# Another order of the mixer's lists: where panel parts stand between small products

## The reference, cut to what matters

```
h = h + W_out [ HGRN2 heads (4) || sliding-window attention (8 query heads) ](RMSNorm(h))   <- the mixer
h = h + CrossAttention_4heads(RMSNorm(h), RMSNorm(mem))
h = h + W_down relu(W_up RMSNorm(h))^2

HGRN2 per head, in chunks of 64 tokens:
  f = lb + (1 - lb) * sigmoid(f_logit);  k = 1 - f
  scores = sum_k q k decay;  o = q S exp(b) + scores v;  S_new = decay S + k^T v
  out = head_rms(o) * silu(g)
Window attention per head: qk-norm, partial rotary, softmax over 256 keys with a sink, times v
```

## The kernel before

| token | TensorE | ScalarE | VectorE |
|---|---|---|---|
| `\|` | next panel part | with part 0 of panel i: copies the high part of panel i+1 (L1152) | nothing |
| `:` | nothing | takes the next panel's result from PSUM (L1119 to L1143) | nothing |
| `T` | 8 transposes, values and keys (L1601, L1606) | copies both (L1205, L1208) | nothing |
| `s0`..`s3` | scores of two chunks (L1632) | nothing | mask, sum (L1424, L1426) |
| `D`, `S` | `D`: state products (L1615) | nothing | `S`: eight state updates, one after another (L1410, L1416) |
| `o0`..`o3` | output of two chunks (L1646, L1648); o3 needs s3's sum | nothing | nothing |
| `q`, `L`, `E` | `L`: total of squares (L1525) | `q`: square (L1214); `L`: root (L1101 to L1108) | `E`: Newton step, gating (L1271, L1273, L1433, L1436) |
| `n`, `r`, `R` | `n`: total (L1525, L1533) | `n`: root | `r`: Newton step (L1469 ff.); `R`: rotation (L1478, L1480) |
| `g0`..`g8` | nothing | g0, g2, g8 in part (L1169 to L1187) | gates and spans; g8 is L1390, L1392 |
| `c0`..`c3` | c0 and c2: window scores of two each (L1685) | exponentials (L1229, L1233) | scale, mask, minimum (L1491) |
| `x0`..`x3` | nothing | nothing | normalization (L1503, L1505, L1508) |
| `w0`..`w3` | four transposes, "turn" (L1697) | copy (L1241) | nothing |
| `p`, `a` | `p`: attention output (L1707) | `a`: copy out (L1247) | nothing |
| `e0`, `e1` | nothing | e0: out gate (L1193 to L1198) | both (L1397 to L1405) |
| `k` | nothing | next block: square (head 1), high part (head 3, L1090) | sum (head 1, L1286), apply (head 2), low part (head 3) |
| `N` | total for the next block's norm (L1583) | root | nothing |
| `V` | transposes of the window's values (L1658) | copy (L1222) | copy |

## Time and profile before

### The profile page before, as it was taken

How to read it: one execution, slowest core, us unless ns; L and a number is a source line. 1 busy time by engine, 2 the same in 40 slices (tenths; PEclk the granted TensorE clock), 3 DMA queues, 4 the chain that set the end, 5 groups by cost and what they waited for, 6 DMA issues and landing times.

```text
span 2652.0 us, 40225 instructions
## 1 busy us (share of the span) xinstructions
PE 2518.6 (95%) x14110; PEld 2035.9 (77%) x14110; DVE 1736.0 (65%) x3014; ACT 1139.5 (43%) x2164; POOL 895.4 (34%) x1018
## 2 busy tenths in 40 slices
PE   7988899899899889989998999999999999999999
PEld 5767677777777667868777888878888888888887
DVE  6778567667766746566656776787666354556665
ACT  5455455555555535644655322342223223322331
POOL 1432200000000055346424766747665222222222
PEclk9999999999999999999999999999999999999999
DMA  4432443353353343164224344323244953444664
GB/s 184 152 113 82 167 131 100 127 175 99 105 192 113 114 159 111 56 232 174 79 88 163 102 137 167 127 96 123 100 138 162 305 169 104 143 132 147 210 187 143
DMA packets 186562, 371.67 MB, mean 140 GB/s; under 512 B 13936, under 2 KB 79984, under 8 KB 183664
## 3 DMA queue, kind: packets, MB, share of 16 engines
q1 hardware_dynamic: 181200, 359.51, 40.7%
q10 hardware_dynamic: 5152, 9.51, 1.0%
HBM read 286.71 MB, written 79.89 MB: 138 GB/s over the span
## 4 chain that ended last, share of the span: by engine, by line
PE 77%; DVE 10%; issue 5%; ACT 5%; DMA 1%; ACTq 0%; POOL 0%; DVEq 0%; SPq 0%; POOLq 0%
PE bank L3236 8%; PE bank L3238 8%; PE bank L3240 8%; PE bank L3216 7%; PE bank L3212 7%; PE bank L3213 6%; PE bank L1549 5%; PE bank L1559 5%; PE bank L1552 5%; PE bank L2161 3%; PE bank L2166 3%; PE bank L2162 3%; PE bank L1632 1%; PE bank L1707 1%; PE bank L2213 1%
## 5 line engine op out<-in xcount | busy, mean ns | idle before, releaser
L454 POOL TENSOR_TENSOR wlo<-raw,whi 128x256 fp32r<-128x256 f32 x372 | 322.4, 898 | 1084.4 <-ACT whi L1156 613.4
L1549 PE MATMUL bank<-hi,whi 128*128 128x512 f32 x704 | 293.0, 416 | 2.0 <-ACT whi L1152 1.8
L1552 PE MATMUL bank<-lo,whi 128*128 128x512 f32 x704 | 278.2, 395 | 0.0
L3238 PE MATMUL bank<-lo,whi 128*128 128x512 f32 x896 | 275.8, 389 | 0.0
L3236 PE MATMUL bank<-hi,whi 128*128 128x512 f32 x896 | 275.8, 389 | 0.0
L3240 PE MATMUL bank<-hi,wlo 128*128 128x512 f32 x896 | 275.8, 389 | 0.0
L3028 DVE TENSOR_TENSOR lo<-h,hi 128x1024 fp32r<-128x1024 f32 x80 | 124.5, 1557 | 172.9 <-ACT hi L2792 172.9
L2723 POOL TENSOR_TENSOR wlo<-h,whi 128x256 fp32r<-128x256 f32 x160 | 127.4, 820 | 299.7 <-ACT whi L2784 299.7
L2161 PE MATMUL bank<-hi,whi 128*128 128x512 f32 x504 | 207.8, 412 | 12.0 <-DVE h L2054 6.4
L2162 PE MATMUL bank<-lo,whi 128*128 128x512 f32 x504 | 196.9, 391 | 0.0
L3238 PEld LDWEIGHTS bank<-lo,whi 128*128 128x128 f32 x896 | 168.2, 188 | 34.9
(11 more groups left out here) (387 smaller groups left out, 5618.3 us busy)
## 6 DMA issues: line engine op xcount, KB each, us to landing
h<-hidden_scratch SPq DMA_DIRECT2D x96, 512.0 KB, 4.2
raw<-w_mix SPq DMA_DIRECT2D x88, 512.0 KB, 4.1
raw<-w_cross SPq DMA_DIRECT2D x64, 512.0 KB, 3.5
raw<-w_mlp SPq DMA_DIRECT2D x64, 512.0 KB, 4.6
wlo<-mixer_lows_scratch SPq DMA_DIRECT2D x60, 512.0 KB, 3.7
hidden_scratch<-hT SPq DMA_DIRECT2D x116, 256.0 KB, 2.1
h<-w_mlp SPq DMA_DIRECT2D x112, 256.0 KB, 3.0
mixer_lows_scratch<-wlo SPq DMA_DIRECT2D x22, 512.0 KB, 2.9
```

What stands on the lines that cost most here:

```text
L454: last = pool.tensor_tensor(wlo[:, i, cols], raw[:, i, cols], whi[:, i, cols].bitcast(F32), ALU.subtract)
L1549: pe.matmul(out, w, hi[:, k, :], start=k == 0, stop=False)
L1552: pe.matmul(out, w, lo[:, k, :], start=False, stop=False)
L3238: pe.matmul(down_bank(i)[:], wh[:, cols], xl[:, i % 2, :], start=False, stop=False)
```

## The change

Tokens move within and between the strings; none is added or taken away. The order of all other steps, the buffers, banks and semaphores stay. Each panel part and each take (`:`) keeps its number, so a part that stands elsewhere is still the next of the 66.

```diff
-    "head 0": "T | s0 s1 | D | n | S | : | r s2 o0 : | e0 R s3 | o1 e1 : o2 | g0 o3 q",
-    "keys": "V | | g1 L E | n r R : | |",
-    "pair 0": "g2 c0 g3 c1 x0 | g4 x1 g5 | | : w0 w1 g6 c2 | : c3 x2 | w2 g7 | x3 w3 e0 | p a g8 : e1 |",
-    "head 1": "T k s0 s1 | | k D n S k k s2 | | : r o0 k | g0 s3 o1 : o2 k k R g1 k o3 q g2 |",
-    "pair 1": "| N c0 c1 g3 | g4 g5 L | : | x0 x1 E w0 | | : w1 g6 g7 | c2 c3 x2 x3 g8 | w2 w3 e0 : p a e1",
-    "head 2": "T | k s0 s1 k | | D n k S | : r | k s2 o0 k | g0 k R s3 : k g1 o1 o2 o3 k q g2 g3 |",
-    "pair 2": "c0 c1 g4 | | L g5 x0 x1 | : | E | g6 : | w0 c2 | c3 w1 g7 x2 g8 | x3 w2 w3 e0 e1 p : a",
-    "head 3": "k T s0 k k s1 k D n k k S s2 k k r o0 o1 | | s3 | | : g0 | g1 | o2 o3 | R q : g2 g3",
-    "pair 3": "c0 x0 g4 | L | : | c1 | E x1 g5 : g6 | w0 | c2 c3 g7 w1 x2 g8 | | x3 w2 w3 : p a",
+    "head 0": "T | s0 s1 | D n | | S | | : r s2 o0 : s3 | e0 | o1 R e1 : o2 g0 | o3 q",
+    "keys": "V | g1 L | E | n r | R : |",
+    "pair 0": "g2 c0 c1 g3 x0 | | x1 g4 g5 | : w0 w1 g6 c2 | : c3 x2 | w2 g7 | x3 w3 | g8 p e0 a : e1",
+    "head 1": "k T s0 k s1 | | | D n S s2 k k | r o0 k : | k | g0 s3 o1 : o2 R k k | o3 q g1 g2",
+    "pair 1": "| N c0 c1 g3 | L | g4 g5 x0 | : x1 E w0 | | g6 : w1 g7 c2 | c3 x2 x3 g8 | w2 w3 e0 | : p a e1",
+    "head 2": "T k | s0 k s1 | D n k k S | : r | s2 o0 k g0 | k R s3 k g1 o1 : g2 o2 o3 k q g3 |",
+    "pair 2": "c0 c1 g4 | | g5 L x0 x1 | | : E | : | g6 w0 c2 w1 | g7 c3 g8 x2 | x3 w2 w3 e0 e1 p a",
+    "head 3": "k T : s0 k k s1 k k D n k S s2 k k r o0 o1 | | s3 | | : g0 | g1 | o2 o3 | R q : g2 g3",
+    "pair 3": "c0 x0 g4 | | L : c1 | | E x1 g5 : g6 | | w0 c2 c3 g7 g8 x2 w1 | | w2 x3 w3 : p a",
```

## The result

The kernel with the changed lists takes 2628.37 us (median of 4 runs, 2624.63 to 2630.76), the kernel before 2653.26 (4 runs beside it, 2648.4 to 2655.76). The ratio is 0.9903, with an interval of 0.989 to 0.9915: 25 us or 1% faster. The forecast was 2628.

What follows compares the result with a forecast made beforehand. TensorE, busy 95% of the span, bounds the kernel, through gaps and stretches at 1.2 GHz. Terms 7.85 + 5.2 + 15.5 - 4.4 = 24.2 us took the profiled 2653.8 to 2629.6, the median to 2628; own range 2620 to 2636, whole range 2618 to 2646.

Steps and rivals of the forecast that it cites:

- Keys: L one part earlier shortens the wait before c0 of pair 0 and keeps the clock up; 7.85 us gained in all.
- Head 1: Waits before o3 and N both go: 1.58 us in turns 0 to 2, 0.45 in turn 3; 5.2 gained.
- Pair 1 and head 2: Earlier c2 and part 12.0 before p remove waits and keep the clock up; 4.94 us in turns 1 and 2, sum 15.5.
- Turn 0: At pair 1, VectorE is late by its own work, so earlier c2 doesn't help; gain 2.0 us, bounds 0.78 and 7.7.
- Pairs 2 and 3: g8 ahead makes w2 wait: 0.5 us a turn lost in pair 2, 0.8 in pair 3; 4.4 lost.
- Head 3: Moving take 16 passes the wait before D on to o0; nothing gained, bounds a gain or loss of 5 us.
- Head 0: No wait stands behind what moves there; put at nothing.
- some 7: Sign to look for: turns 1 and 2 should each be some 7 us shorter.
- The falls move: Clock falls come at up to seven pair ends of pairs 2 and 3, 2.60 us each; 2646 us, chance 0.20.
- The other engines absorb it: VectorE or ScalarE set the pace, waits come back later; 5.2 us gained, 2647 us, no change, chance 0.12.
- Slower, by small products joined: Clock falls at p T s0 s1 and between w2 and p, 4 + 7 places; 2663 us, chance 0.06.

Runs made afterwards that it cites:

- early strings alone: The changed kernel with the strings of pair 2, head 3 and pair 3 as they were before; 2624.82 us, ratio 0.9897 to the kernel before.
- the take alone: The kernel before with only take 16 moved behind ScalarE's copies for T of head 3; 2652.02 us, ratio 0.9995.
- both edits of pair 1: The kernel before with c2 of pair 1 ahead of part 11.1 and part 12.0 between w3 and p; 2638.01 us, ratio 0.9936.
- the late strings: The kernel before with only the strings of pair 2, head 3 and pair 3 as in the changed one; 2659.83 us, ratio 1.0032.
- the kernel with two parts: The early strings alone plus one more panel part between w2 and w3 of pair 1, taken from head 2; 2620.48 us, again 2621.05.

## Why the prediction was right

**What bounds.** TensorE with its gaps and its clock: shown. The gain in turn 2 is about half of the one and half of the other, and the whole kernel has the same 14110 products.

**Keys.** Right in mechanism, small in size: forecast 2.9 in turns 1 and 2, measured 3.1. The wait fell to 0.15 and not to 0.6. The chain moved ahead by 1.5 us and not 1.35: `L` starts 0.94 us after the weight copy's start, before 2.48. ScalarE in order of time in turn 2 of the changed kernel:

```profile
545.49 1.06 ACT L1152 ACTIVATE whi<-raw 128x1024 fp32r<-128x1024 f32 x1
546.43 0.70 ACT L1101 ACTIVATE mean<-bank,eps 128x512 f32<-128x512 f32 x1
```

**Head 1.** Forecast 1.58 in turns 0 to 2, measured 1.7 in 1 and 2, in the changed kernel and alone. In turn 0 it measured 2.4 alone, for the longer wait there, and 1.5 in the changed kernel, where `w2` of pair 0 has a new wait of 0.72.

**Pair 1 and head 2.** Forecast 4.94, measured 5.3. The pair of experiments shows the parts: the earlier `c2` takes the 1.56 and the fall (4.4), the part between `w3` and `p` the 0.78 and, alone, half of the fall or all of it. In turn 3 it is 3.9, forecast 3.64. Turn 0 is the term that was mis-sized: forecast a gain of 2.0, measured 0.95 up to `D` of head 2, and behind it 1.5 lost, which the forecast didn't have. There `o3` of head 2 waited 1.59 us before and waits longer now, and the clock falls behind it, where it didn't. TensorE, turn 0 of the changed kernel:

```profile
220.65 0.34 PE L1646 MATMUL bank<-qdec,st 128*64 128x64 f32 x4 [1.89 <-DVE hs L1426]
```

The sum of turn 0 came near its 3.0 all the same (2.0), since the keys gave 1.6 there and not 0.7. That is luck.

**Pairs 2 and 3.** Forecast a loss of 0.5 and 0.8 a turn; measured 0.45 and 0.7 in turn 2, and as a whole 2.5 to 3.6 us (whole change against early strings alone) where 4.4 was forecast.

**Head 3.** Forecast nothing, measured -1.05 and +1.15 with the take alone; in the changed kernel -1.05 and +0.55, half a microsecond of gain. The stretch behind `D` varies by more than this (23.65 to 25.26 us in turn 2) among kernels in which head 3 is as before.

**Head 0.** Put at nothing; from `T` to `V` it is 0.5 us shorter in turn 2. Of this 0.42 lies between `D` and `V` (19.68 and now 19.26), without a wait and at a clock of 1.00 in both, and every profile with the changed string has it. No run had this string alone, so which of its moves does it stays open.

**Sum.** In turn 2 the terms measure 3.1 + 1.7 + 5.3 + 0.5 (head 0) + 0.5 (head 3) - 0.45 - 0.7 = 9.95, against the 10.05 of the whole turn and the 8.1 of the forecast ("some 7" among its signs). The mixer gained 28.2 and not 24.2, and the 2.4 us that the preparation and the stretch from cross attention on took back brought the total next to the forecast. So the 2628 is nearer than its terms were, by luck. By the ratios of the runs, keys (10.6), both edits of pair 1 (17.0), head 1 (8.6, a single execution) and the late strings (-8.5) add up to 27.7 us, the whole change to 25.7.

**The rivals.** *The falls move* was partly so. The changed kernel has one at pair 2 in turn 3 that before has not:

```profile
870.50 3.56 PE L1707 MATMUL bank<-pT,vsw 128*64 128x128 f32 x32 [0.78 <-ACT pT L1241]
```

Its second profile has none there, but one at the end of pair 3 in turn 2. That is one new fall among the seven pair ends in each, not all. *The other engines absorb it* fell, with the exception of head 3, where it is what happens. *Slower, by small products joined* fell: `p T s0 s1` and the ends of pair 1 run at 1.00 in turns 1 and 2.

## What to carry to other kernels

Where long work (here panel parts) can stand anywhere, put it where a small cluster waits for another engine, and look first at the wait that the clock's fall follows: here a wait of 1.56 us cost 4.4. Follow an operation that is moved ahead to the next thing that waits for the same engine: take 16 moved a wait of 1 us by one step and saved nothing. Do one group of strings at a time: of this change a third of the strings cost 2.5 to 3.6 us, and leaving them out was better than the whole.

## What the runs showed of the hardware

**One wait, two outcomes.** Before `c0` of pair 0 a wait of 1.60 us left the clock up and one of 1.93 didn't; with both edits of pair 1, whose list leaves this place as it was, 1.93 did both. TensorE in turns 1 and 2 of that kernel:

```profile
351.45 1.13 PE L1685 MATMUL bank<-ksw,qk 64*128 64x256 f32 x8 [1.93 <-issue]
...
559.27 1.90 PE L1685 MATMUL bank<-ksw,qk 64*128 64x256 f32 x8 [1.93 <-issue]
```

and in turn 0 of others 2.28 stayed up where 2.29 fell (above). So the length of the wait doesn't decide alone, and what does isn't shown. A single profile's turn 0 therefore can't be put down to an edit: it took between 222.95 and 234.81 us in kernels whose lists differ by little. Part of this is only its start, which a fall in the preparation puts off: `T` stands at 76.69 to 79.94 us.

**Falls repeat, up to a point.** The two profiles of the changed kernel have their first nine falls, from 81.9 to 679.2 us, at the same times to 0.1 us. Then they part: one has a fall at 720.1, the other at 870.4. The two profiles of the kernel with two parts part at once: one has a fall at 62.8 us, where the clock is 1.00 in the other. Yet the falls that both have there begin at the same times to 0.1 us, too (192.5 and 192.6, 257.4 and 257.5, 298.3 and 298.4). The Trainium skill, "TensorE: Matmul & The Clock Gate", section "What's actually happening", has the monitor running freely, not in step with the kernel. The trace agrees as far as that which falls there are differs between executions of one kernel; that they begin at other times it doesn't show, and two pairs are few.

**More work, no more time.** Eight products whose results nobody reads, 1.8 us of work ahead of a wait of 2.83, made the kernel no slower: it was 2.0 us ahead within 30 us, and 3.6 at its end, which isn't clear of noise. From the first product of cross attention to the first with `W_down`, where the program is the same in all kernels, it took 1094.3 to 1099.9 us from profile to profile; this wasn't taken apart, and some of the 2 to 4 us between the fastest kernels may be it.
